# Another order of work in the attention stage of a two-block network on one core: values later, turned in another bank, roots and vector items in other steps

## The reference

```python
q = rms_norm(split_heads(h @ w_q), q_gain)      # 16 heads of 64
k = rms_norm(split_heads(h @ w_k), k_gain)
v = split_heads(h @ w_v)
kc = rms_norm(split_heads(hc @ w_k), k_gain)    # 256 context tokens
vc = split_heads(hc @ w_v)
s = concat([q @ k_window * scale + bias, q @ kc * scale])
p = softmax(s)
y = (p[window] @ v_window + p[ctx] @ vc) @ w_o
```

## Time and profile before

| | |
|---|---|
| runs | 2659.39, 2667.57, 2669.72 us, median 2667.57 |
| profiled execution | 2667.07 us, span 2665.2 us |
| TensorE busy | 2487.8 us, 93% of the span |
| VectorE, ScalarE, GpSimd busy | 61%, 31%, 39% |
| granted TensorE clock, mean | 0.974 |

### The profile page before, as it was taken

One profiled execution on the slowest core, in us unless ns is written; L12 is line 12 of the kernel. 1 busy time (PEld: TensorE's weight loads), 2 busy tenths in 40 slices (PEclk: granted clock), 3 DMA queues, 4 the chain that ended last, 5 costly groups with the idle time before them and its releaser, 6 DMA issues.

```text
span 2665.2 us, 32621 instructions
## 1 busy us (share of the span) xinstructions
PE 2487.8 (93%) x11368; PEld 2014.9 (76%) x11368; DVE 1634.9 (61%) x1793; ACT 815.0 (31%) x1076; POOL 1044.9 (39%) x456
## 2 busy tenths in 40 slices
PE   6789999989999987999999899998799898799999
PEld 4677888868888876778888688886567676588887
DVE  7964155477666868712545767669866665773534
ACT  3132222222222221422222322222376764332222
POOL 3314444434444432344444344444122323244443
PEclk9999999999999998999999999999799999899999
DMA  4212223233434221123222333333011111222322
GB/s 157 79 32 95 95 95 102 95 121 100 140 137 141 96 79 62 63 87 98 99 95 94 126 138 99 142 135 112 28 38 46 48 36 55 72 99 90 103 89 92
DMA packets 64440, 247.24 MB, mean 93 GB/s; under 512 B 7152, under 2 KB 9584, under 8 KB 63088
## 3 DMA queue, kind: packets, MB, share of 16 engines
q1 hardware_dynamic: 62064, 218.92, 24.7%
q10 hardware_dynamic: 2304, 27.38, 2.7%
HBM read 244.17 MB, written 2.10 MB: 92 GB/s over the span
## 4 chain that ended last, share of the span: by engine, by line
PE 73%; DVE 17%; DVEq 5%; ACT 3%; issue 2%; DMA 0%; ACTq 0%
PE ps L468 69%; DVEq L1483 2%; DVE E L1130 2%; ACT prob L1014 1%; DVE C_lo_f L1279 1%; DVE C_lo L1114 1%; DVE E L1126 1%; DVE A_hi L1112 1%; DVEq L1273 1%; DVE A_lo L1114 1%; DVE k_hi L1112 1%; DVE H_lo_f L1138 1%; DVE C_hi L1112 1%; DVE H_lo_f L1431 1%; DVEq L1125 1%
## 5 line engine op out<-in xcount | busy, mean ns | idle before, releaser
L421 POOL TENSOR_TENSOR w_lo<-w_raw,w_hi 128x1024 fp32r<-128x1024 f32 x404 | 1010.6, 2504 | 1579.6 <-ACT w_hi L863 1561.7
L468 PE MATMUL ps<-H_hi,w_hi 128*128 128x512 f32 x1952 | 780.8, 400 | 33.7 <-DVE H_lo L1437 14.6
L468 PE MATMUL ps<-H_hi,w_lo 128*128 128x512 f32 x1952 | 766.0, 392 | 0.0
L468 PE MATMUL ps<-H_lo,w_hi 128*128 128x512 f32 x1952 | 765.7, 392 | 0.0
L863 ACT ACTIVATE w_hi<-w_raw 128x1024 fp32r<-128x1024 f32 x401 | 422.8, 1057 | 841.0 <-PE ps L468 798.7
L468 PEld LDWEIGHTS ps<-H_hi,w_hi 128*128 128x128 f32 x1952 | 369.5, 189 | 132.6 <-issue 44.9
L468 PEld LDWEIGHTS ps<-H_hi,w_lo 128*128 128x128 f32 x1952 | 369.9, 189 | 78.8
L468 PEld LDWEIGHTS ps<-H_lo,w_hi 128*128 128x128 f32 x1952 | 370.5, 190 | 76.6 <-issue 3.6
L468 PE MATMUL ps<-A_hi,w_hi 128*128 128x512 f32 x560 | 221.4, 395 | 5.8 <-DVE A_lo L1114 4.2
L468 PE MATMUL ps<-A_lo,w_hi 128*128 128x512 f32 x560 | 219.3, 392 | 0.0
L468 PE MATMUL ps<-A_hi,w_lo 128*128 128x512 f32 x560 | 219.1, 391 | 0.0
(11 more groups left out here) (214 smaller groups left out, 3111.9 us busy)
## 6 DMA issues: line engine op xcount, KB each, us to landing
w_raw<-weights SPq DMA_DIRECT2D x404, 512.0 KB, 3.5
mod_w<-mod_weights ACTq DMA_DIRECT2D x8, 3072.0 KB, 10.8
X<-x SPq DMA_DIRECT2D x4, 512.0 KB, 6.5
out<-X SPq DMA_DIRECT2D x8, 256.0 KB, 2.0
toeplitz<-biases SPq DMA_DIRECT2D x14, 128.0 KB, 2.0
decay_sb<-decay ACTq DMA_DIRECT2D x1, 1024.0 KB, 7.6
ctx_sb<-context SPq DMA_DIRECT2D x1, 1024.0 KB, 5.5
mask_sb<-key_mask ACTq DMA_DIRECT2D x1, 320.0 KB, 2.7
```

Of the source, the lines that this page charges most:

```text
L421: nc.gpsimd.tensor_tensor(w_lo[:, q, :], w_raw[:, q, :], w_hi[:, q, :].bitcast(F32), ALU.subtract).then_inc(w_lo_ready, 1)
L468: mm = nc.tensor.matmul(dst, w[l], xs[r], start=start and a == 0, stop=stop and a == 2)
```

## The change

The same instructions are issued, in another order on TensorE, ScalarE and VectorE, with other semaphore waits to suit. Per tile t, the projections of q and v move one to two steps later, the turn of the values goes to step 3 (part 0) and the next step 0 (part 1) and into `TURN_BANK`, and roots, casts of weights and vector items stand in other steps. The core of the diff:

```diff
@@ turn_values
                 if part == 0:
-                    pe.wait_ge(vt_ready, 2 * T + 2)
-                    pe.wait_ge(root_ready["q"], T + 1)
+                    pe.wait_ge(vt_ready, T + 1)
+                    pe.wait_ge(vt_ctx_ready, T + 1)
+                    pe.wait_ge(pt_ready, 2 * STEPS * T)
                 else:
                     pe.wait_ge(v_ready, 2 * T + 1)
+                    pe.wait_ge(pt_ready, 2 * STEPS * T + 2)
...
-                    mm = nc.tensor.transpose(ps[:, SUM_BANK, c * P:(c + 1) * P], src, ident_sb[:, :])
+                    mm = nc.tensor.transpose(ps[:, TURN_BANK, c * P:(c + 1) * P], src, ident_sb[:, :])
@@ turn
+                T, i = divmod(g, STEPS)
+                if i < 2 and head == 0:
+                    pe.wait_ge(v_ready, 2 * T + i + 1)
@@ TensorE, ahead of the tiles
-            dense(0, "v", 0, DT)
+            dense(0, "v", 0, 4)
             head_sums(0, "q")
+            dense(0, "v", 4, DT)
             dense_ctx(0, "k")
-            dense(1, "k", 0, 4)
+            dense(1, "k", 0, 3)
             head_sums(0, "kc")
-            dense(1, "k", 4, DT)
+            dense(1, "k", 3, 6)
             dense_ctx(0, "v")
+            scores(0)
+            dense(1, "k", 6, 7)
             turn_values(0, 0)
-            dense(1, "q", 0, 2)
-            turn_values(0, 1)
+            dense(1, "k", 7, DT)
             dense_ctx(1, "k")
-            scores(0)
-            dense(1, "q", 2, 3)
-            head_sums(1, "kc")
             head_sums(1, "k")
-            dense(1, "q", 3, 5)
@@ TensorE, between the two turns of a step
                     if T < TILES:
                         if p == 0:
-                            dense(T, "q", 5, 7)
+                            dense(T, "q", 0, 2)
                         if p == 1:
-                            dense(T, "v", 3, 5)
-                    if after < TILES:
+                            dense(T, "v", 0, 2)
                         if p == 2:
-                            dense(after, "k", 2, 4)
+                            dense(T, "v", 4, 6)
+                    if p == 3 and after < TILES:
+                        dense(after, "k", 5, 7)
...
@@ TensorE, behind scores(g + 1) (and weigh)
                         if p == 0:
-                            dense(T, "q", 7, DT)
+                            head_sums(T, "kc")
+                            dense(T, "q", 2, DT)
+                            turn_values(t, 1)
+                        if p == 1:
+                            head_sums(T, "q")
                             dense_ctx(T, "v")
-                            head_sums(T, "q")
-                            dense(T, "v", 0, 3)
-                        if p == 1:
-                            dense(T, "v", 5, DT)
+                            dense(T, "v", 2, 4)
                         if p == 2:
+                            dense(T, "v", 6, DT)
+                        if p == 3:
                             turn_values(T, 0)
                     if after < TILES:
-                        if p == 1:
-                            dense(after, "k", 0, 2)
                         if p == 2:
-                            dense_ctx(after, "k")
-                            turn_values(T, 1)
-                            dense(after, "k", 4, DT)
+                            dense(after, "k", 0, 5)
                         if p == 3:
-                            head_sums(after, "kc")
+                            dense(after, "k", 7, DT)
+                            dense_ctx(after, "k")
                             head_sums(after, "k")
-                            dense(after, "q", 2, 5)
...
+                        if p == 0:
+                            turn_values(t, 1)
+                            output(2, 1, 5)
@@ ScalarE
                     copy_turned(g, 0)
-                    if p == 3 and after < TILES:
-                        squares(after, "kc")
-                        squares(after, "k")
                     copy_turned(g, 1)
-                    if p == 0 and T < TILES:
+                    if p == 0:
+                        if t == 0:
+                            act.wait_ge(ctx_mm, 2)
+                        ahead_at(ATT_JOB + 3 * after)
+                    if p == 1 and T < TILES:
                         squares(T, "q")
+                    if p == 2 and T < TILES:
+                        act.wait_ge(ctx_mm, 2 * T + 1)
+                        ahead_at(ATT_JOB + 3 * after + 1)
                     if g + 1 < TILES * STEPS:
                         for head in range(2):
                             exponential(g + 1, head)
+                        if p == 3 and after < TILES:
+                            squares(after, "k")
                         for head in range(2):
                             divide(g + 1, head)
+                    if p == 3 and after < TILES:
+                        squares(after, "kc")
                     if p == 0 and T < TILES:
+                        head_roots(T, "k")
+                        head_roots(T, "kc")
+                    if p == 1 and T < TILES:
                         head_roots(T, "q")
-                    if p == 3 and after < TILES:
-                        head_roots(after, "kc")
-                        head_roots(after, "k")
-                    if T < TILES and p < 3:
-                        if t == 0 and p == 0:
-                            act.wait_ge(ctx_mm, 2)
-                        ahead_at(job_of(after, "k") + p)
...
+                    if p == 2 and T < TILES:
+                        ahead_at(ATT_JOB + 3 * after + 2)
@@ VectorE
-                    if T < TILES:
-                        if p == 0:
-                            item_scaled(T, "kc")
-                            item_split(T, "kc")
-                        if p == 2:
-                            values_out(T)
+                    if p == 2 and T < TILES:
+                        item_scaled(T, "q")
                     if g + 1 < TILES * STEPS:
                         least(g + 1)
-                    if T < TILES and p == 2:
+                    if p == 0:
+                        values_turned(t, 1)
+                    if p == 2 and T < TILES:
+                        values_out(T)
+                    if p == 3 and T < TILES:
                         values_turned(T, 0)
                     if g + 1 < TILES * STEPS:
                         inverses(g + 1)
-                    if T < TILES:
-                        if p == 0:
-                            item_scaled(T, "k")
-                            item_split(T, "k")
-                        if p == 1:
-                            item_scaled(T, "q")
-                            item_split(T, "q")
-                        if p == 2:
-                            values_turned(T, 1)
+                    if p == 1 and T < TILES:
+                        item_scaled(T, "k")
+                        item_split(T, "k")
+                        item_scaled(T, "kc")
+                        item_split(T, "kc")
+                    if p == 2 and T < TILES:
+                        item_split(T, "q")
```

More of the change, by code:

```diff
@@ L735, in output @@
                         pe.wait_ge(sq_ready["q"], TILES)
-                    else:
-                        pe.wait_ge(vt_ready, 2 * TILES)
+                    if m == 1:
+                        pe.wait_ge(vt_ready, TILES)
+                    if m == 2:
+                        pe.wait_ge(vt_ctx_ready, TILES)
                     if m == 3:
-                        pe.wait_ge(v_ready, 2 * TILES)
+                        pe.wait_ge(root_ready["q"], TILES)
                 for k in range(first, last):
@@ L776, in _ @@
                         if p == 0:
-                            dense(T, "q", 5, 7)
+                            dense(T, "q", 0, 2)
                         if p == 1:
-                            dense(T, "v", 3, 5)
-                    if after < TILES:
+                            dense(T, "v", 0, 2)
                         if p == 2:
-                            dense(after, "k", 2, 4)
-                        if p == 3:
[L784 to L795, removed]
+                            dense(T, "v", 4, 6)
+                    if p == 3 and after < TILES:
+                        dense(after, "k", 5, 7)
+                    if p == 3 and after == TILES:
+                        output(0, 4, 6)
+                    if T == TILES:
+                        if p == 0:
+                            output(1, 5, 6)
+                            output(2, 0, 1)
+                        if p == 1:
+                            output(2, 5, 6)
+                            output(3, 0, 1)
+                        if p == 2:
+                            output(3, 3, 4)
+                        if p == 3:
+                            output(2, 6, 7)
                     turn(g, 1)
@@ L811, in _ @@
                         if p == 2:
+                            dense(T, "v", 6, DT)
```

(46 more changed lines are left out.)

13 lines of the change are left out of this document (7 added, 6 removed).

## The result

The changed kernel takes 2708.5 us (median of 4 runs, 2702.62 to 2710.16), the kernel before 2665.93 us (median of 4). The ratio is 1.0158, with a 95% interval of 1.0132 to 1.0184: slower by 42.6 us between the medians, 1.6%. The profiled execution took 2708.43 us, its span is 2706.6 us against 2665.2.

What follows compares the result with a forecast made beforehand. TensorE, busy 93% of the span, was taken as the bound. Seven tiles' waits and clock, 83.3 us, plus 2.5 and 0.9, less 34.8, gave +51.9; another count +48; taken +49: 2716 us, range 2690 to 2736.

Steps and rivals of the forecast that it cites:

- waits at the turns of values: TensorE's waits behind VectorE's copy `vt_ctx`, 17.5 us before the change; the 2.22 us wait of a middle tile goes.
- A: Start of step 1: TensorE idles 1.8 us per tile because the inverses queue behind the late copy of values.
- B: Second turn of step 1: TensorE idles 1.7 us per tile; copy `pt` queues behind ScalarE's division, table load and roots.
- C: Start of step 3: TensorE idles 6.4 us per tile, 4.1 without `low`, because VectorE's k, kc, q delay step 2's `least`.
- clock behind C: Slow products on TensorE in step 3 after each long wait there, priced at 2.0 us per tile.
- prologue, last tile: Ends of the attention stage: 0.9 us waiting for kc at `scores(0)`, and 2.5 us of small waits in the last tile.
- rival in which kc escapes the `low`: VectorE's cast of kc avoids GpSimd's `low` before step 3: wait of 4.1 us, 16 less in all, 2700 us; chance 0.22.
- rival in which A and B, 1.8 us apart, lower the clock as well: Step 1's two waits together cost clock, or more collisions occur: 11 to 18 us more, 2727 to 2734; chance 0.15.
- the 34.8 at stake: Attention stage before the change: 30.6 us of waits it can touch, plus 1.6 and 2.6 us of lost clock.
- rival "faster": Inverses not held by `values_turned`, step 2's `least` on time: new loss 10.1 us against 34.8, 2642 us; chance 0.02.

Runs made afterwards that it cites:

- k in step 0: Changed kernel with VectorE's whole item of k moved from behind step 1's inverses to behind step 0's: 2665.48 us, ratio 1.0011 to the kernel before.
- three edits: Changed kernel with step 0's inverses before the values' copy, k's item behind that copy, q's weights cast in step 0: 2633.23 us, ratio 0.9893.

## Why the prediction was right

Forecast 2716 us within 2690 to 2736; measured 2708.5. The direction, the three places and their causes held, and the errors of size all go one way, a little too large; no error made up for another:

| step | as predicted | measured |
|---|---|---|
| waits at the turns of values | gone | none listed |
| A, seven times | 1.8 | 1.47 |
| B, seven times | 1.7 | 1.51 |
| C, seven times | 6.4 with `low`, 4.1 without | 5.71 (four), 6.08 (two), 6.39; 3.7 to 4.4 without |
| clock behind C | 2.0 a tile | 1.0 to 2.3 (24.97 to 26.33 us from step 3's first turn to step 1's second, against 23.98 with k in step 0, where the clock is 1.00) |
| prologue, last tile | 0.9, and 2.5 | 0.9, and 1.0 (with the 0.7 that both kernels have, 1.7) |

- *A and B.* The cause was as stated, copy ahead of inverses. Undoing only that order took 14.7 us off. What I priced as one wait A is two things stacked: 0.74 us of bank handover, and the rest the delayed inverses. The prices were better than the table shows, since I counted from start to start and the profile counts idle from the end of the last record. From start to start the turn of values comes 1.96 us ahead of the turn of probabilities (predicted 2.0), and the second turn 4.33 us behind the first division (predicted 4.3).
- *C.* `least` of step 2 starts 14.56 us behind the start of k; the sum said 12.6 + 2.3. I had the `low` hit the cast of kc; in the tile shown it hits the split behind it, at the same price; it is so in five tiles, and the cast in two. The cast escaped by 0.02 us there, and it made no difference, because the split was next. The rival in which kc escapes the `low` occurred in none of the seven tiles, and its price was right: 2.3 predicted, 2.0 measured when the `low` is moved away.
- *Clock.* That every wait C would be followed by a slow stretch held: 0.52 over the 2.93 us behind one, 0.50 to 0.58 behind all seven. Its price of 2.0 was too high on average: 1.4 over the first six. One reason is that I set the 3.39 us of the earlier trace rows against 1.83, and a turn and six products behind a wait take 2.13 us even at full clock (with k in step 0). The rival in which A and B, 1.8 us apart, lower the clock as well is refuted by the window that begins at the end of A and ends 4.8 us behind B (1.00), and by the version with k in step 0, whose whole tile is at 1.00.
- *The sum.* The rows give 7 x (1.47 + 1.51) + 41.4 + 7 x 1.9 = 75.6, and 1.9 for the ends: 77.5 us, less the 34.8 at stake: +42.7, against the 42.6 between the medians and 41.4 between the spans. The 1.9 is the busy time of six tiles above 37.63; 1.4 of it is clock, and the other 0.5 belongs to the three waits, as above. In this count the terms that were too large are A and B (24.5 against 20.9), C (44.8 against 41.4), the last tile (2.5 against 1.0) and the clock (14.0 against 13.3 of longer busy time). Counted from start to start, as I had priced them, A and B are right to 0.1 us, and the clock and C carry the excess. With seven tiles, a third of a us in each wait makes 2.3.
- *The rival "faster"* did not occur in the changed kernel, but named the mechanism rightly: it needs both the inverses before the copy and `least` on time. With both (three edits) the new waits are 7 x 0.74 and small ends, and the stage is 28.7 us shorter than before the change; the rival's sum gave 24.7.

## What to carry to other kernels

When a schedule is rewritten by hand, look in each engine's list for an item whose input comes late and read what stands behind it: a copy of 0.6 us in front of two 0.16 us inverses cost 14.7 us here, and taking one of three items out of the row in front of a minimum gave back 37.6. The slack to spend is in the step where the engine is idle: VectorE stood idle for 3.8 us in front of the copy and for 5.9 in front of step 1's `least`, and was then 5.7 us late for step 3. Taking a wait away shows what is late next: put off q, and the scores wait; move k, and the `low` holds q's scaling instead of the split of kc. So judge by the time of the whole tile, and from start to start, since short waits don't show in the list of waits.

## What the hardware showed that I had not expected

- A cast that began 0.02 us ahead of GpSimd's `low` kept its 0.29 us, while the split that began 0.34 us behind it took 2.45 instead of 0.42. With k in step 0 the operation caught is q's scaling, 2.53 us instead of 0.75. The Trainium skill (SBUF — State Buffer, Who interferes with whom) has the first to start keep the port pair; the rows agree.
- Three waits of 1.47, 1.51 and 1.74 us in one tile left the granted clock at 1.00. Those of 5.7 us and more took it to the 1.2 GHz level, but for unequal times: 1.0 us lost in one tile, 2.3 in another. With q behind the inverses, the same two waits of 1.62 and 3.10 us lowered it in one tile (0.96) and not in the tile before it (1.00).
- The stage starts up to 10 us sooner or later (1898.9 to 1908.5 us) in executions of kernels that are the same up to there, and the runs of one kernel lie as far apart (2664.34 to 2674.00 us with k in step 0). That is nearly a quarter of the effect studied, and it comes from outside the edit; why is not shown.
